# A fourth tile of 128 tokens takes its experts by gathers, and the dense 512 tokens become one span

## The chip, the cores and the metric

The kernel runs on one core of a Trainium2 chip. The metric is the time of one execution on the device, in microseconds (us); the median of the runs counts. A profile of one execution comes with it.

## The reference

One step of an encoder layer for 1024 prompt tokens and 32 sample tokens (1056 together), model width 1024, in fp32. It has sparse and forgetting attention, cross-attention into 256 memory tokens, and at the end a mixer that looks up experts, which is the part that the change touches:

```python
def peer_ffn(xn, w_q, keys1, keys2, u, v):      # cut
    def blk(xb):                                 # xb: 128 tokens
        q = (xb @ w_q).reshape(TOK_BLOCK, 8, 256)
        s1 = einsum('thd,hnd->thn', q[..., :128], keys1)   # 8 heads x 128 keys
        s2 = einsum('thd,hnd->thn', q[..., 128:], keys2)
        v1, i1 = top_k(s1, 16);  v2, i2 = top_k(s2, 16)
        ...                                      # the best 16 of the 256 pairs, per head
        eidx = ...                               # i1 * 128 + i2: one of 16384 experts
        g = softmax(sv)
        h = gelu(einsum('td,thkd->thk', xb, u[eidx]), approximate=False)
        return einsum('thk,thkd->td', g * h, v[eidx])
```

So each token picks 8 x 16 = 128 experts. An expert is one row of 1024 numbers in `u` and one in `v`; both tables have 16384 rows (64 MB each).

## The kernel before

The mixer computes the same thing in two ways. For the *dense* tokens TensorE multiplies all 16384 experts, 128 at a time (a *chunk*; there are 128 chunks), and a gate that is zero for the experts that a token did not pick weighs the result. For the *sparse* tokens GpSimd gathers, for each token, the 128 rows that it picked, by one indirect DMA (128 rows x 4 KB = 0.524 MB) from `u` and later one from `v`. Three tiles of 128 prompt tokens and the 32 sample tokens are sparse. The sample tokens are laid out four ways, so that 32 tokens x 128 experts take 32 gathers as well, and `NSP` = 3 x 128 + 32 = 416 gathers are made from each table. The other `ND` = 640 tokens are dense, and TensorE takes them in two spans (`NGD` = 2) of `TD` = 320 columns.

Operands of the dense products are split in two fp32r parts, and three matmuls (`PRODUCTS`) stand for one. Per chunk and span that is 8 x 3 = 24 matmuls.

Four stages matter, with each engine running its own instruction list, all tied by semaphores:

1. `peer_queries` computes the queries. At its end ScalarE and GpSimd split the dense columns of the normed input into `xd` (L1254, L1217).
2. `route` (1757 to 2788 us). Nine tiles in the order `ORDER` (sparse ones and the sample tile first) go through VectorE, which picks the best 16 keys and pairs in 20 ordered steps. Meanwhile TensorE works on the dense hidden values (`DenseHidden`): SyncE loads a chunk of `u` (0.524 MB) into one of two buffers (`load`), ScalarE rounds it (`round`, L1310), GpSimd subtracts to get the low part (`split`, L1314), TensorE multiplies (`product`, L1326), ScalarE applies Gelu (L1337), SyncE stores the result to `s_hid`. Also meanwhile GpSimd gathers rows of `u` into 8 row buffers (`gather`, L1567) and VectorE makes a dot product of each row set with the token (`dot`, L1598), in nine slots between its first steps of a tile. `CHUNKS_AT[j]` and `DOTS_AT[j]` say how many chunks and dots stand beside tile j. GpSimd's list for a tile is, per chunk, one split and then gathers up to a goal that is 4 ahead of an even spread. In the last chunk of stage j ScalarE first waits for VectorE's tile j - 1 (`dd_ready`, `Exp` at L1543), and TensorE waits for its indices at the end of the stage (`turn`, L1480), so the lists meet once per tile. Gathers begin in stage 2, after the chunks of stages 0 and 1. After the last `Exp`-marked tile 32 dots remain.
3. `spread_gates` (2788 to 3065 us, with the last store landing near 3097). For each dense token VectorE makes two one-hot matrices (L1916, L1921), TensorE multiplies them to a 128 x 128 gate (L1879), ScalarE copies four tokens at a time to `g_stage` (L1934), SyncE stores 128 tokens at once (8.4 MB) to `s_gate`. There are two stage buffers. Beside it the first 24 batches (`B_STEPS`) of the sparse sum run: GpSimd gathers four token rows of `v` (L1788), TensorE adds them (`SparseSum.sum`, L1821: 16 matmul records a batch).
4. `experts` (3115 to 4268 us). 32 phases of four chunks. SyncE loads `v`, the stored hidden values and the gates of a chunk (two buffers each); ScalarE and GpSimd round and split `v` (L2101, L2142); VectorE multiplies hidden by gate (L2176), ScalarE rounds, VectorE splits (L2181). These run one phase ahead of TensorE, which multiplies four outputs at a time over the four chunks (L2080) into four PSUM banks; VectorE adds them to `y` (L2216). Between groups TensorE takes the remaining 80 batches of sparse rows (L1821), at positions from `slot_of`. GpSimd gathers those rows (L1788) into `NBUF` = 11 buffers, two batches ahead of the sums.

## Time and profile before

| | us |
|---|---|
| median of 3 runs (4300.76 to 4316.1) | 4309.61 |
| the profiled execution | 4316.03 |
| its span, first to last instruction | 4314.1 |

| engine | busy us | share of the span |
|---|---|---|
| TensorE, matmul (PE) | 3830.1 | 89% |
| TensorE, weight load (PEld, beside PE) | 3166.4 | 73% |
| VectorE (DVE) | 2510.5 | 58% |
| ScalarE (ACT) | 995.8 | 23% |
| GpSimd (POOL) | 1604.4 | 37% |

The DMA engines moved 835.35 MB, of which 436.26 MB in the queue that GpSimd's gathers use and 371.29 MB in that of SyncE's direct DMAs. Busy shares are averages over the whole span; the stages have different limits. Times in rows are from the start of the span. A matmul's record lasts longer than the distance to the next one, since matmuls are pipelined: distances, not durations, give its cost. A few records are missing in the trace. PEclk 1.00 is the full clock of 2.4 GHz, 0.50 is 1.2 GHz.

### The profile page before, as it was taken

How to read it: one execution, taken by the hardware profiler on the slowest of the kernel's cores; microseconds unless marked ns; L12 is line 12 of the kernel's file. 1: busy time of each engine (PE TensorE's matmuls, PEld its weight loads, DVE VectorE, ACT ScalarE, POOL GpSimd, SP SyncE). 2: the span in 40 equal slices, each digit the busy share in tenths (PEclk: the TensorE clock that was granted, in tenths of full speed). 3: DMA queues.
4: the chain of work that ended last, by engine and by line, in shares of the span. 5: the costliest groups of instructions: out<-in, count | busy, mean ns of one | idle time of the engine just before them, and what ended most of it. 6: DMA issues, size and time to landing. Idle time of an engine off the chain costs nothing. (4 is left out here: it accounts for less than half of the span.)

```text
span 4314.1 us, 61852 instructions
## 1 busy us (share of the span) xinstructions
PE 3830.1 (89%) x22675; PEld 3166.4 (73%) x22691; DVE 2510.5 (58%) x6016; ACT 995.8 (23%) x1843; POOL 1604.4 (37%) x1134
## 2 busy tenths in 40 slices
PE   7878888888899989899999999787499999999996
PEld 4445665665567689899999999765378888888885
DVE  3878883330124142489999989898444544444444
ACT  1213332330102010322222222233222211211121
POOL 0000000000000033377777778646265655555551
PEclk9889998999999999999999999899799999999998
DMA  2010000003110132499999899789887887787772
GB/s 102 13 48 17 16 7 10 10 13 135 49 49 11 34 114 79 138 340 336 329 331 339 320 357 386 298 280 348 271 304 280 304 289 287 277 295 277 278 278 97
DMA packets 334637, 835.35 MB, mean 194 GB/s; under 512 B 28496, under 2 KB 130776, under 8 KB 332480
## 3 DMA queue, kind: packets, MB, share of 16 engines
q0 software_dynamic: 119808, 436.26, 26.9%
q1 hardware_dynamic: 210128, 371.29, 24.8%
q10 hardware_dynamic: 4464, 24.66, 1.4%
q8 instruction: 147, 2.41, 0.2%
q14 instruction: 90, 0.74, 0.1%
HBM read 722.74 MB, written 109.36 MB: 193 GB/s over the span
## 5 line engine op out<-in xcount | busy, mean ns | idle before, releaser
L2080 PEld LDWEIGHTS e_y_ps<-e_wh,e_vh 128*128 128x128 f32 x6144 | 918.3, 191 | 180.6 <-issue 94.2
L2080 PE MATMUL e_y_ps<-e_wh,e_vh 128*128 128x320 f32 x6144 | 953.8, 315 | 100.0 <-DVE e_wh L2181 60.3
L1326 PE MATMUL h_ps<-xd,h_uh 128*128 128x320 f32 x6144 | 925.0, 312 | 2.1 <-POOL h_uh L1314 2.0
L1326 PEld LDWEIGHTS h_ps<-xd,h_uh 128*128 128x128 f32 x6144 | 916.3, 191 | 5.8 <-POOL h_uh L1314 5.0
L1209 POOL CAST q_wh<-q_w 128x1024 fp32r<-128x1024 f32 x16 | 18.4, 1148 | 1634.8 <-DMA q_w<-in_w_pq 1528.6
L2216 DVE TENSOR_TENSOR oT<-e_y_ps,oT 128x320 f32<-128x320 f32 x512 | 231.6, 486 | 612.7 <-PE e_y_ps L2080 511.7
L1598 DVE CUSTOM_DVE_ANT_0 oT<-oT,r_row_ps 128x1024 f32<-128x1024 f32 x416 | 490.8, 1215 | 115.9 <-DMA oT<-in_u,eid 97.7
L2142 POOL TENSOR_TENSOR e_vh<-e_v,e_vh 128x1024 fp32r<-128x1024 f32 x128 | 318.8, 2493 | 449.7 <-ACT e_vh L2101 448.7
L1567 POOL DMA_INDIRECT oT<-in_u,eid x416 | 410.9, 988 | 123.6 <-issue 97.1
L1314 POOL TENSOR_TENSOR h_uh<-h_u,h_uh 128x1024 fp32r<-128x1024 f32 x128 | 327.5, 2559 | 180.4 <-ACT h_uh L1310 172.1
L197 PE MATMUL m_ps<-oT,m_w 128*128 128x352 f32 x1152 | 346.2, 464 | 21.1 <-DVEq L203 20.5
L1788 POOL DMA_INDIRECT e_rows<-in_v,idt x320 | 319.6, 999 | 91.7 <-issue 75.5
L197 PEld LDWEIGHTS m_ps<-oT,m_w 128*128 128x128 f32 x1152 | 221.0, 192 | 145.4 <-DVEq L203 21.9
L1337 ACT ACTIVATE h_hid<-h_ps 128x320 f32<-128x320 f32 x256 | 111.2, 437 | 626.2 <-PE h_ps L1326 492.3
L2106 ACT ACTIVATE e_wh<-e_hid 128x640 fp32r<-128x640 f32 x128 | 94.2, 737 | 627.3 <-DVE e_hid L2176 589.9
L1879 PE MATMUL g_ps<-g_hot 128*128 128x128 f32 x1280 | 177.2, 288 | 51.1 <-DVE g_hot L1921 50.5
L1879 PEld LDWEIGHTS g_ps<-g_hot 128*128 128x128 f32 x1280 | 154.7, 193 | 89.1 <-DVE g_hot L1921 66.3
L1236 PE MATMUL q_ps<-q_xh,q_wh 128*128 128x352 f32 x1152 | 186.0, 324 | 11.3 <-POOL q_wh L1211 11.3
L1236 PEld LDWEIGHTS q_ps<-q_xh,q_wh 128*128 128x128 f32 x1152 | 185.8, 190 | 11.8 <-issue 11.8
L1788 POOL DMA_INDIRECT oT<-in_v,idt x96 | 148.9, 1551 | 109.8 <-PE z_ps L1821 87.1
L2176 DVE TENSOR_TENSOR e_hid<-e_hid,e_gate 128x640 f32<-128x640 f32 x128 | 146.9, 1148 | 60.8 <-DMA e_gate<-s_gate 60.8
L1921 DVE TENSOR_SCALAR g_hot<-con,routes 128x128 f32<-128x128 f32 x640 | 179.9, 360 | 0.0
(272 smaller groups left out, 4768.5 us busy)
## 6 DMA issues: line engine op xcount, KB each, us to landing
h_u<-in_ut SPq DMA_DIRECT2D x128, 512.0 KB
e_v<-in_v SPq DMA_DIRECT2D x128, 512.0 KB
s_hid<-h_hid SPq DMA_DIRECT2D x128, 320.0 KB
s_gate<-g_stage SPq DMA_DIRECT2D x5, 8192.0 KB
e_hid<-s_hid SPq DMA_DIRECT2D x128, 320.0 KB
e_gate<-s_gate SPq DMA_DIRECT2D x128, 320.0 KB
s_pq<-q_out ACTq DMA_DIRECT2D x16, 528.0 KB, 2.7
q_w<-in_w_pq SPq DMA_DIRECT2D x16, 512.0 KB, 3.5
```

What stands on the lines that cost most here:

```text
L197: mm = pe.matmul(self.ps[:, b * n + g, 0:c], self.wbuf[:, b, k, :], self.src[:, k, a:a + c], start=(k == 0), stop=(k == KD - 1))
L1236: mm = pe.matmul(ps[:, b, g, 0:TG], wh[:, b, hw, k * P:(k + 1) * P], xh[:, hx, k, g * TG:(g + 1) * TG], start=(k == 0 and n == 0), stop=(k ...
L1314: pool.tensor_tensor(self.uh[:, n % 2, LO, :], self.u[:, n % 2], self.uh[:, n % 2, HI, :].bitcast(F32), ALU.subtract).then_inc(self.split_ ...
L1326: mm = pe.matmul(self.ps[:, bank % 3, 0:TD], self.uh[:, n % 2, a, k * P:(k + 1) * P], self.xd[:, b, k, g * TD:(g + 1) * TD], start=(k == 0 ...
L1567: pool.indirect_dma_start(out=rows[:, n % N_ROW, :], out_offset=None, in_=dram["u"], in_offset=bass.IndirectOffsetOnAxis(ap=eid[:, n:n + 1 ...
L1598: dve.tensor_tensor_reduce(out=rows[:, d % N_ROW, :], in0=rows[:, d % N_ROW, :], in1=row_flat, scale=1.0, scalar=0.0, op0=ALU.mult, op1=AL ...
L1788: pool.indirect_dma_start(out=buffer, out_offset=None, in_=self.rows_dram, in_offset=bass.IndirectOffsetOnAxis(ap=self.idt[:, col:col + 1] ...
L1879: mm = pe.matmul(ps[:, q % 4, x, :], hot2[:, q % 4, x, :], hot1[:, q % 4, x, :], start=True, stop=True)
L1921: op = dve.tensor_scalar(hot1[:, g, x, :], iota, routes[:, 0, tok], routes[:, 2, tok], ALU.is_equal, ALU.mult)
L2080: mm = pe.matmul(y_ps[:, o, 0:TD], vh[:, n % SLOT, a, m * P:(m + 1) * P], wh[:, n % SLOT, b, g * TD:(g + 1) * TD], start=(c == 0 and e == ...
L2142: pool.tensor_tensor(vh[:, n % SLOT, LO, :], v[:, n % 2, :], vh[:, n % SLOT, HI, :].bitcast(F32), ALU.subtract).then_inc(v_split, 1)
L2216: dve.tensor_tensor(y[:, m, cols], y_ps[:, o % 4, 0:TD], y[:, m, cols], ALU.add).then_inc(y_added, 1)
```

## The change

`NS` goes from 3 to 4: a fourth tile of 128 prompt tokens is sparse. 512 dense tokens are left, and they form one span of 512 columns (`TD, NGD = ND, 1`), so that each weight is used by one matmul of 512 columns where two of 320 used it. There are 544 gathers from each table instead of 416: 128 more dots in `route`, and 112 instead of 80 batches of the sparse sum in `experts` (the 24 in `spread_gates` stay). `route` gets new lists: stages 2 to 9 have 14 chunks each, stages 1 to 8 have 64 dots each. `spread_gates` makes four stores instead of five; the stage buffers change places, so that the first store goes into buffer 1. The turned weights of the sample tokens go to a PSUM bank of their own, since 544 columns don't fit in one, and ScalarE copies them by two instructions. In `experts` there are 8 outputs in a phase instead of 16, VectorE adds two per chunk (was four), the sums of sparse rows may follow every second chunk of a group, and `NBUF` is 13.

```diff
-NS = 3
+NS = 4
 C0 = NS * P
 ND = T_P - C0
-TD, NGD = ND // 2, 2
+TD, NGD = ND, 1
...
-CHUNKS_AT = (2, 6, 13, 13, 13, 13, 13, 13, 17, 17, 8)
+CHUNKS_AT = (3, 10, 14, 14, 14, 14, 14, 14, 14, 14, 3)
-DOTS_AT = (0, 43, 43, 42, 43, 43, 42, 64, 64, 32)
+DOTS_AT = (0, 64, 64, 64, 64, 64, 64, 64, 64, 32)
...
-            act.wait_ge(self.kept, 1)
+            act.wait_ge(self.kept, 2)
...
-        assert NB % 2 == 1
-        keep["gates_stored"] = (stored[0], 16 * (NB // 2 + 1))
+        assert NB % 2 == 0
+        keep["gates_stored"] = (stored[1], 16 * (NB // 2))
...
-                             stage[:, n % 2]).then_inc(stored[n % 2], 16)
-            sp.wait_ge(stored[1], 16 * (NB // 2))
+                             stage[:, 1 - n % 2]).then_inc(stored[n % 2], 16)
+            sp.wait_ge(stored[0], 16 * (NB // 2))
...
-                    mm = pe.matmul(sums.ps[part, 1, 0, C0:NSP], hn[:, C0:NSP], ident[:, part],
+                    mm = pe.matmul(sums.ps[part, 1, 1, 0:T_S], hn[:, C0:NSP], ident[:, part],
...
-                act.activation(stage[:, n % 2, :, q % NQ * 4:q % NQ * 4 + 4], ps[:, q % 4].rearrange("p x a -> p a x"),
+                act.activation(stage[:, 1 - n % 2, :, q % NQ * 4:q % NQ * 4 + 4], ps[:, q % 4].rearrange("p x a -> p a x"),
                                ACT.Copy).then_inc(copied, 1)
...
-                    act.activation(sums.wt[:, :], sums.ps[:, 1, 0, 0:NSP], ACT.Copy).then_inc(sums.kept, 1)
+                    act.activation(sums.wt[:, 0:C0], sums.ps[:, 1, 0, 0:C0], ACT.Copy).then_inc(sums.kept, 1)
+                    act.activation(sums.wt[:, C0:NSP], sums.ps[:, 1, 1, 0:T_S], ACT.Copy).then_inc(sums.kept, 1)
...
-NBUF = 11
+NBUF = 13
...
-                    for s in steps_in(p, b0 // 4):
-                        if s in TURNS:
-                            turn_sum(TURNS.index(s))
-                        else:
-                            sparse_sum(batch_at(s))
+                        if c % 2 == 0:
+                            continue
+                        for s in steps_in(p, b0 // 2 + c // 2):
+                            if s in TURNS:
+                                turn_sum(TURNS.index(s))
+                            else:
+                                sparse_sum(batch_at(s))
...
-                    for o in range(4 * i, 4 * i + 4):
-                        if p + 1 < NPH and o == 4 * i:
+                    for o in range(2 * i, 2 * i + 2):
+                        if p + 1 < NPH and o == 2 * i:
                             weigh(n)
-                        if p + 1 < NPH and o == 4 * i + 2:
+                        if p + 1 < NPH and o == 2 * i + 1:
                             split(n)
```

## Rows read from the trace of the kernel before

**Rows 1.** Stretches: us, busy time (count) of each engine, PEclk, DMA share, GB/s.

```profile
1757.40:2788.50 1031.10, 954.76 (x6427) 948.56 (x6427) 909.88 (x2805) 280.33 (x454) 738.39 (x546) 0.96 0.88 325
2788.50:3065.30 276.80, 224.78 (x1678) 165.99 (x1678) 258.96 (x795) 97.74 (x175) 147.41 (x95) 0.97 0.88 304
3115.20:4268.00 1152.80, 1102.79 (x7489) 958.81 (x7489) 518.81 (x773) 226.39 (x292) 628.76 (x444) 0.98 0.76 277
```

**Rows 2.** Timeline of ScalarE, the routing tiles' marks: start us, us, instruction, idle before.

```profile
1919.83 0.31 ACT L1543 ACTIVATE r_eg<-r_dd 128x128 f32<-128x128 f32 x1 [11.33 <-DVE r_dd L1691]
...
2442.37 0.31 ACT L1543 ACTIVATE r_eg<-r_dd 128x128 f32<-128x128 f32 x1 [11.66 <-DVE r_dd L1691]
...
2579.14 0.31 ACT L1543 ACTIVATE r_eg<-r_dd 128x128 f32<-128x128 f32 x1 [14.86 <-DVE r_dd L1691]
...
2713.85 0.31 ACT L1543 ACTIVATE r_eg<-r_dd 128x128 f32<-128x128 f32 x1 [15.00 <-DVE r_dd L1691]
```

**Rows 3.** Waits from 2579 to 2713.8: us in total, times, longest us.

```profile
POOL h_uh L1314 <- ACT h_uh L1310: 11.2, 1, 11.2
```

**Rows 4.** Groups by line, routing stage: count | busy us, mean ns | idle before.

```profile
L1567 POOL DMA_INDIRECT oT<-in_u,eid x416 | 410.9, 988 | 123.6 <-issue 97.1 <-DVE hn L1598 22.0
L1314 POOL TENSOR_TENSOR h_uh<-h_u,h_uh 128x1024 fp32r<-128x1024 f32 x127 | 325.2, 2560 | 159.8 <-ACT h_uh L1310 151.5 <-issue 6.9
```

**Rows 5.** Timeline: gate stage of VectorE, and ScalarE's first expert row.

```profile
3051.94 0.69 DVE L1916 TENSOR_TENSOR g_hot<-con,routes 128x512 f32<-128x512 f32 x1
...
3053.56 0.69 DVE L1916 TENSOR_TENSOR g_hot<-con,routes 128x512 f32<-128x512 f32 x1
...
3097.66 1.06 ACT L2101 ACTIVATE e_vh<-e_v 128x1024 fp32r<-128x1024 f32 x1 [32.39 <-DMA e_v<-in_v]
```

**Rows 6.** Timeline of the expert stage, TensorE: three groups of 48 and two sums.

```profile
3311.37 14.56 PE L2080 MATMUL e_y_ps<-e_wh,e_vh 128*128 128x320 f32 x96
3325.86 1.92 PE L1821 MATMUL z_ps<-e_rows,z_wz 128*32 128x512 f32 x16
...
3336.91 0.41 PE L2080 MATMUL e_y_ps<-e_wh,e_vh 128*128 128x320 f32 x1
```

**Rows 7.** Timeline of the routing stage, ScalarE: one chunk's two Gelus.

```profile
2494.77 0.44 ACT L1337 ACTIVATE h_hid<-h_ps 128x320 f32<-128x320 f32 x1 [2.19 <-PE h_ps L1326]
2498.23 0.44 ACT L1337 ACTIVATE h_hid<-h_ps 128x320 f32<-128x320 f32 x1 [3.02 <-issue]
```

**Rows 8.** A stretch of the query stage, L1236 alone (352 columns): PE, PEld, PEclk, DMA.

```profile
1540.00:1580.00 40.00, 40.00 (x253) 40.00 (x253) 1.00 0.27 93
```

**Rows 9.** Timeline of VectorE in routing: a tile's end and eight dots.

```profile
2578.82 0.28 DVE L1691 TENSOR_TENSOR r_dd<-r_sv 128x128 f32<-128x128 f32 x1
...
2601.20 1.20 DVE L1598 CUSTOM_DVE_ANT_0 oT<-oT,r_row_ps 128x1024 f32<-128x1024 f32 x1
...
2610.31 0.08 DVE L1662 MATCH_VALUE_LOAD r_pick<-r_v,r_s 128x8 f32 x1
```

**Rows 10.** Stretches as in rows 1: a routing tile in two parts, gates, experts' start.

```profile
2578.00:2604.00 26.00, 25.04 (x152) 24.73 (x153) 25.49 (x46) 8.51 (x15) 19.42 (x11) 0.88 0.60 205
2604.00:2702.00 98.00, 97.81 (x663) 96.86 (x662) 87.55 (x291) 25.75 (x41) 83.08 (x67) 1.00 1.02 400
2850.00:2990.00 140.00, 120.74 (x928) 88.22 (x920) 140.00 (x432) 52.32 (x95) 82.92 (x57) 1.00 1.08 381
3110.00:3130.00 20.00, 7.08 (x24) 6.34 (x24) 4.22 (x4) 2.10 (x3) 1.16 (x1) 0.50 0.80 305
```

**Rows 11.** The gathers of routing, one line: duration ns min/median/max, first and last start us.

```profile
L1567 POOL DMA_INDIRECT oT<-in_u,eid x416: 932/938/2212, 1828.6 to 2775.8; - x139
```

**Rows 12.** Waits of the gate stage: us in total, times, longest us.

```profile
DVE g_hot L1916 <- PE g_ps L1879: 15.9, 1, 15.9
```

**Rows 13.** Groups by line, whole span, expert stage: columns as in rows 4.

```profile
L1788 POOL DMA_INDIRECT e_rows<-in_v,idt x320 | 319.6, 999 | 91.7 <-issue 75.5 <-PE z_ps L1821 9.6
L2142 POOL TENSOR_TENSOR e_vh<-e_v,e_vh 128x1024 fp32r<-128x1024 f32 x128 | 318.8, 2493 | 449.7 <-ACT e_vh L2101 448.7
```

## Prediction

> **What bounds the kernel now.** I read the busy time of each engine by stage first [rows 1]. The edit touches three stages: the routing stage (1757.4 to 2788.5 us), the gate stage (to 3065.3) and the expert stage (3115.2 to 4268.0). TensorE is busy 93% and 96% of the first and last, so narrow views have to say whether it is also what sets their pace.
>
> Routing works in tiles; one `Exp` on ScalarE marks each [rows 2]. Tiles with 42 or 43 dot products and 13 chunks are 104.5 us apart (five intervals between the first two rows), the two with 64 and 17 are 136.8 and 134.7 us apart. Inside the last one GpSimd waits only once, 11.2 us [rows 3]; a gather costs it 0.988 + 0.276 = 1.26 us (mean duration, and 97.1 us of issue gaps over 352), a weight split 2.56 us [rows 4]. 17 x 2.56 + 64 x 1.26 + 11.2 = 135.4 us: GpSimd's queue alone gives the measured tile. The 11.2 us lie between its last gather of a tile and the next split: rows land, VectorE finishes the dots, then `Exp`, Gelu and the rounding on ScalarE. TensorE waits for VectorE there too. In 13-chunk tiles GpSimd needs 33.3 + 54 + 11 = 98 us and TensorE about as much, and 104.5 us come out.
>
> In the gate stage VectorE never rests: its step for 4 tokens repeats every 1.63 us [rows 5]. The expert stage is TensorE's: 8.5 us per slot of 48 matmuls and 2/3 of a row sum [rows 6].
>
> **Change, routing stage.** Each tile now has 64 dots and 14 chunks.
> - TensorE: 48 matmuls of 320 columns become 24 of 512. Gelu follows Gelu by 3.46 us in the rows shown and by 3.52 on average of a chunk's two, per 24 matmuls [rows 7]: 146.5 ns each. 253 matmuls of 352 columns fill 40 us: 158 ns [rows 8]. That slope (0.36 ns a column) gives 216 ns at 512, one cycle a column of 2.4 GHz gives 226; I take 226, as both rows sit 11 to 13 ns above their columns. A chunk falls from 7.04 to 5.42 us.
> - GpSimd: 14 x 2.56 + 64 x 1.26 + 11.2 = 127.7 us a tile.
> - VectorE: eight dots from 2601.20 to 2610.31, 1.14 us each, 73 us; the rest of a tile about 48 us, of which 22.4 stand in one piece without dots (2578.8 to 2601.2) [rows 9]. 121 us.
> - DMA: 64 gathers x 0.524 MB + 14 x (0.524 + 0.262) + 1.05 = 45.6 MB. The engines carry 400 GB/s for the 98 us in which dots run, and 5.3 MB in the 26 us around the piece without dots [rows 10]. 26 + 40.3/0.400 = 127 us.
>
> Three resources lie within 7 us of each other, and TensorE, with 76 + 13 us, is out. I take 128.5 us a tile, bounds 125 and 136 (the 17-chunk tiles, whose sum met the measured time without a surplus).
>
> Gathers begin once 14 chunks instead of 9 are through: 14 x 5.42 against 9 x 7.04 us, +12.5, with one more tile of x rows turned first (8 matmuls and a copy) +14.5: first gather at 1843 instead of 1828.6 [rows 11]. From it to the first tile's `Exp` took 91.2 us [rows 2]; 20 more gathers and a split make it 119, so 1962. Seven tiles x 128.5 end at 2861.5. Then 19 us of VectorE without dots, 32 dots x 1.14, 5 of waits, 3.3 to the next stage: 64, so 2925.5. **Routing: +137 us** (bounds +112, +190).
>
> **Change, gate stage.** 160 steps become 128. VectorE: 32 x 1.63 = -52. But the 96 gathers stay and are squeezed: a batch of four (2.1 MB) every 4.5 steps, 7.3 us, is 286 GB/s, and this stage saturates at 381 [rows 10]; 95 are left for the stores of 8.4 MB, one per 52 us. All bytes (83.9 MB) less the 10 of the first 52 us need 194 us, so 246 us; VectorE's chain with the last store (27 us) needs 235. From the stage's start to the first expert row now: 310 us (to 3098) [rows 5], with one wait of 15.9 us of VectorE in it [rows 12], behind a late gather. I take 250: **-60 us** (bounds -68, -40).
>
> **Change, expert stage.**
> - TensorE: 144 matmuls and 2 sums take 25.5 us, a sum 1.86 us, so 151 ns a matmul [rows 6]. Now 6144 x 0.151 + 80 x 1.86 + 10 = 1087 of 1152.8 us. After: the overhead above the columns (17.7 ns) kept, 231 ns: 3072 x 0.231 + 112 x 1.86 + 12 = 930.
> - GpSimd: 448 gathers x 1.24 + 124 splits x 2.49 = 865 us (now 706) [rows 13].
> - DMA: gathers 235 MB, v 67, hidden and gates 67, y 4: 373 MB (now 323 at 280 GB/s). At 400 GB/s 932 us.
> - VectorE: 128 weigh/split pairs at (0.61 + 0.69) and 256 adds at 0.6: 320 us. No bound. In a group of four outputs its order (add, split, add, weigh, add, split, add, 4.4 us from the first output, which is there 2.05 us before the group's end) is some 0.4 us late for the fourth bank; a sum in between covers it in most groups.
>
> So 932, 930 and 865 replace one leader with 1087. Today's loss above the leader is 66 us, about 20 of it the cold start. Where three were equal before (13-chunk tiles, 98 each) 7% came on top. 930 x 1.07 + 20 = 1015; DMA has to hold 92% of its best rate here if nothing else stalls, more than in any tile, so I take 1031 (362 GB/s on average, what the 17-chunk tiles held). **-122 us** (bounds -200 at the floors, -35 if DMA averages 335 GB/s as in the 13-chunk tiles).
>
> The ring of 13 rows (was 11) and the moved PSUM columns cost nothing; `xd` splits are shorter by 2.4 us before the stage, hidden by the extra turned tile.
>
> The Trainium skill (DMA: Bandwidth & Descriptors, Specifications) gives a core a limit of about 358 GB/s at the HBM. The 400 GB/s over 98 us, mostly reads of tables there, stand against it [rows 10]. By the rule the expert stage could not be under 373/0.358 = 1042 us, the total not under 4276, and case A below could not be.
>
> **Sum.** Profiled execution 4316.0 us: +137 - 60 - 122 = -45, 4271. The median shown is 6.4 below that execution: 4265.
>
> **Rivals.**
> A. The expert stage overlaps nearly ideally (950 to 990 us). For: thirteen row buffers and a phase of slack between load and use. Taken at 970: 4265 - 61 = 4204.
> B. Slower: DMA decides the expert stage. TensorE waits in order for gathered rows between dense groups; in the trace no sum of that stage waits for DMA, at 76% DMA share, so nothing shows how it behaves near 100%. Each late batch delays the dense groups, their release of v and hidden buffers, and so the next loads. At 335 GB/s the stage takes 1114 us: 4348. It decides from 343 GB/s downwards (1088 us, at which the total is 4322, 0.3% slower).
> C. Routing tiles stay at 135 to 136 us, because VectorE's two-input steps stretch GpSimd's gathers and DMA waits add: +52, 4317, no change.
> D. TensorE's clock. In routing it would be busy 5.4 of every 8.3 us. At 86% busy in the gate stage it is granted 2.4 GHz, at 35% (3110 to 3130) 1.2 [rows 10]; between them no row speaks. At 1.2 GHz a chunk takes about 10.3 us and a tile 158: +235 us, 4500. Against: a slow chunk keeps TensorE busy without a gap. The Trainium skill (TensorE: Matmul & The Clock Gate, A second HAM failure mode: psum-queue depth-cycling) tells of a kernel in which short pauses between groups of matmuls let the clock swing between its levels; by that this case would come, in part at least.
>
> **How the numbers follow.** Forecast case (4215 to 4295) 0.47; A 0.16; B 0.17; C 0.13; D 0.03; 0.04 unforeseen. 0.3% is about what a measurement can tell from no change. A and the forecast and a part of C are faster: 0.69. C's rest and the edges: same 0.12. B, D and what is unforeseen: slower 0.19. Range 4190 to 4345: it takes in A and most of B, and leaves out D and the worst of B.
>
> **What would show it.** `Exp` marks 126 to 131 us apart and the first at 1962; gate-stage matmuls starting near 2926; expert stage 1000 to 1065 us with a DMA share above 0.9 and TensorE waiting for gathered rows; matmuls of 512 columns 226 to 231 ns apart. Wrong, if tiles are 121 or 136 us, or if the expert stage is under 1000 or over 1088 us.

## The result and the profile after

The changed kernel takes 4364.5 us (median; 4362.0 to 4368.2), the kernel before 4310.0 beside it. The ratio is 1.0139 (95% interval 1.0120 to 1.0158): it is 1.4% slower, where 4265 was forecast, and outside the range. Its profiled execution took 4365.3 us with a span of 4363.3.

Both spans divide at the same marks: first dense matmul of the routing stage, first matmul of the gate stage, first dense matmul of the expert stage, last one.

| stage, us | before | after | difference | forecast |
|---|---|---|---|---|
| routing | 1031.1 | 1192.8 | +162 | +137 |
| gates, to the first expert matmul | 326.7 | 284.6 | -42 | -60 |
| experts | 1151.8 | 1079.8 | -72 | -122 |
| sum | | | +48 | -45 |

So the median lies 99 us above the forecast: 50 of them are in the expert stage, 25 in routing, 18 in the gates; the rest is mostly that this profiled execution lies 0.8 us above its median, where the forecast took 6.4 off.

The first view is busy time by stage, as in [rows 1] (start:end, length, then busy us and instructions of PE, PEld, DVE, ACT, POOL, and PEclk, DMA share, GB/s): routing, the gate stage's matmuls, 10 us inside them, the expert stage, and last the seven routing tiles between first and last `Exp`.

```profile
1758.80:2951.60 1192.80, 857.94 (x3356) 663.04 (x3356) 1075.28 (x3042) 246.97 (x327) 855.10 (x675) 0.87 0.88 330
2951.60:3186.00 234.40, 196.11 (x1424) 139.30 (x1424) 207.66 (x635) 77.69 (x143) 117.43 (x95) 0.93 0.91 323
3070.00:3080.00 10.00, 2.26 (x11) 2.29 (x11) 0.06 (x1) 2.25 (x5) 0.00 (x0) 0.50 1.08 342
3236.20:4316.00 1079.80, 1025.17 (x4944) 637.98 (x4944) 356.88 (x518) 220.13 (x309) 735.08 (x572) 0.99 0.91 342
1964.05:2887.40 923.35, 665.43 (x2566) 510.99 (x2565) 866.49 (x2451) 189.98 (x251) 685.56 (x546) 0.87 0.91 343
```

In the last row VectorE is busy 94% of the tiles, TensorE 72%, GpSimd 74%, and no engine is at 100%. In the expert row TensorE is busy 1025 of 1080 us, yet the floor forecast for its work was 930. A matmul that waits once it has begun counts as busy: the records of the sums (L1821) fill 291 us of this row, and 226 in lead3 below, where the same sums find their rows.

The tiles' marks, answering to [rows 2]: (2887.41 - 1964.05) / 7 = 131.9 us a tile.

```profile
1964.05 0.31 ACT L1543 ACTIVATE r_eg<-r_dd 128x128 f32<-128x128 f32 x1 [21.32 <-DVE r_dd L1691]
...
2887.41 0.31 ACT L1543 ACTIVATE r_eg<-r_dd 128x128 f32<-128x128 f32 x1 [20.82 <-DVE r_dd L1691]
```

Groups of the page, answering to [rows 4] and [rows 13]: count | busy us, mean ns | idle before and its releaser.

```profile
L1567 POOL DMA_INDIRECT oT<-in_u,eid x544 | 538.4, 990 | 185.8 <-issue 119.8
L1788 POOL DMA_INDIRECT e_rows<-in_v,idt x448 | 438.4, 979 | 119.7 <-issue 106.5
...
L2145 POOL TENSOR_TENSOR e_vh<-e_v,e_vh 128x1024 fp32r<-128x1024 f32 x128 | 306.3, 2394 | 247.7 <-ACT e_vh L2104 246.1
L1314 POOL TENSOR_TENSOR h_uh<-h_u,h_uh 128x1024 fp32r<-128x1024 f32 x128 | 316.4, 2472 | 166.1 <-ACT h_uh L1310 164.3
```

GpSimd's prices are close to the forecast's (gathers 0.98 to 0.99 us, splits 2.4 to 2.5). So its counts and prices were right, and what came on top is order and waiting. The waits from 3180 to 4320 us (us in total, times, longest us) name the first such thing.

```profile
POOL e_vh L2145 <- ACT e_vh L2104: 246.1, 59, 46.4
...
PEld z_ps L1821 <- DMA e_rows<-in_v,idt: 104.8, 76, 2.6
...
PE z_ps L1821 <- DMA e_rows<-in_v,idt: 44.5, 51, 1.7
...
POOL e_rows L1788 <- PE z_ps L1821: 5.5, 18, 0.3
```

TensorE's weight loads wait for gathered rows in 76 places, 104.8 us in total. The 51 waits of its matmuls begin at the same moments and are the same waits, so they are not added (the 149 us of the expectation of lead3 counts them twice). Before, no wait of that stage was for rows. GpSimd, which issues these gathers, hardly waits for a free row buffer (5.5 us), but 246 us for ScalarE's rounding, 198 of them inside the stage. The chain of waits of 80 us in mid-stage (start, us, what) shows how the two hang together:

```profile
3516.32 2.03 PE z_ps L1821 x16
...
3518.38 0.24 ACT z_wz L1802
...
3518.78 1.05 ACT e_vh L2104
...
3519.90 2.40 POOL e_vh L2145
...
3522.44 0.95 POOL e_rows L1788
...
3527.43 2.40 POOL e_vh L2145
...
3532.75 0.94 POOL e_rows L1788
...
3533.99 9.42 DMA e_rows<-in_v,idt
...
3543.45 1.90 PE z_ps L1821 x10
3545.36 5.71 PE e_y_ps L2081 x24
```

A sum ends at 3518.35. ScalarE had waited for it, since after every fourth batch it places the weights of a later four; its next instruction rounds `v`, GpSimd splits that, gathers a batch, splits again, gathers the next, and that one's last row lands 9.4 us later, at 3543.41. From the end of the sum to the landing 25.1 us pass. The row belongs to the third sum after. TensorE's own timeline there (start, us, what, [idle before]):

```profile
3516.25 2.09 PE L1821 MATMUL z_ps<-e_rows,z_wz 128*32 128x512 f32 x16
...
3523.93 2.74 PE L1821 MATMUL z_ps<-e_rows,z_wz 128*32 128x512 f32 x16
...
3532.27 2.68 PE L1821 MATMUL z_ps<-e_rows,z_wz 128*32 128x512 f32 x16
...
3540.57 1.96 PE L1821 MATMUL z_ps<-e_rows,z_wz 128*32 128x512 f32 x6
3543.45 1.90 PE L1821 MATMUL z_ps<-e_rows,z_wz 128*32 128x512 f32 x10 [0.92 <-DMA e_rows<-in_v,idt]
3545.29 5.78 PE L2081 MATMUL e_y_ps<-e_wh,e_vh 128*128 128x512 f32 x24
3550.99 1.92 PE L1821 MATMUL z_ps<-e_rows,z_wz 128*32 128x512 f32 x16
3552.85 5.78 PE L2081 MATMUL e_y_ps<-e_wh,e_vh 128*128 128x512 f32 x24
```

Where nothing waits, a sum follows the last one after 7.6 us (3543.45 to 3550.99: 1.85 for the sum, 5.70 for 24 dense matmuls). So between the end of a sum and the fourth row of the third sum after TensorE has three dense groups, two sums and three eighths of one, 21.5 us of work, and the row comes after 25.1. The missing 3.6 us are waits. As an estimate from these rows, 28 such rounds of four batches lose 28 x 3.6 = 101 us. In the kernel before, the same three sums lie 39 to 46 us apart (for example sums at 3623.04 and 3661.95).

### The profile page after: what moved, and what is told of

Same layout as the page of the kernel before. It is cut to its first block and busy times, and to the rows that moved or that the text cites. A ratio compares the mean times of both kernels' runs of the same rounds, so it can differ in the third digit from the quotient of the medians.

```text
span 4363.3 us, 50039 instructions
## 1 busy us (share of the span) xinstructions
PE 3640.8 (83%) x16837; PEld 2539.1 (58%) x16837; DVE 2466.6 (57%) x5860; ACT 937.3 (21%) x1703; POOL 1795.1 (41%) x1390
## 5 line engine op out<-in xcount | busy, mean ns | idle before, releaser
L1326 PE MATMUL h_ps<-xd,h_uh 128*128 128x512 f32 x3072 | 826.9, 430 | 183.1 <-POOL h_uh L1314 183.1
L1326 PEld LDWEIGHTS h_ps<-xd,h_uh 128*128 128x128 f32 x3072 | 629.1, 208 | 372.3 <-POOL h_uh L1314 222.3
L2081 PE MATMUL e_y_ps<-e_wh,e_vh 128*128 128x512 f32 x3072 | 742.4, 397 | 59.9 <-DVE e_wh L2184 56.2
L2081 PEld LDWEIGHTS e_y_ps<-e_wh,e_vh 128*128 128x128 f32 x3072 | 570.1, 189 | 279.0 <-issue 133.7
L1598 DVE CUSTOM_DVE_ANT_0 oT<-oT,r_row_ps 128x1024 f32<-128x1024 f32 x544 | 641.2, 1215 | 112.2 <-DMA oT<-in_u,eid 106.7
L1567 POOL DMA_INDIRECT oT<-in_u,eid x544 | 538.4, 990 | 185.8 <-issue 119.8
L1788 POOL DMA_INDIRECT e_rows<-in_v,idt x448 | 438.4, 979 | 119.7 <-issue 106.5
L2219 DVE TENSOR_TENSOR oT<-e_y_ps,oT 128x512 f32<-128x512 f32 x256 | 175.7, 687 | 519.2 <-PE e_y_ps L2081 519.2
L1821 PE MATMUL z_ps<-e_rows,z_wz 128*32 128x512 f32 x1792 | 291.1, 606 | 44.7 <-DMA e_rows<-in_v,idt 44.5
L2179 DVE TENSOR_TENSOR e_hid<-e_hid,e_gate 128x512 f32<-128x512 f32 x128 | 115.7, 904 | 237.9 <-DMA e_gate<-s_gate 237.9
L1236 PE MATMUL q_ps<-q_xh,q_wh 128*128 128x352 f32 x1152 | 186.1, 324 | 11.3 <-POOL q_wh L1211 11.3
L1236 PEld LDWEIGHTS q_ps<-q_xh,q_wh 128*128 128x128 f32 x1152 | 185.8, 190 | 11.8 <-issue 11.8
L1821 PEld LDWEIGHTS z_ps<-e_rows,z_wz 128*32 128x32 f32 x1792 | 58.6, 109 | 212.5 <-issue 106.7
```

The source lines that it names most:

```text
L1236: mm = pe.matmul(ps[:, b, g, 0:TG], wh[:, b, hw, k * P:(k + 1) * P], xh[:, hx, k, g * TG:(g + 1) * TG], start=(k == 0 and n == 0), stop=(k ...
L1326: mm = pe.matmul(self.ps[:, bank % 3, 0:TD], self.uh[:, n % 2, a, k * P:(k + 1) * P], self.xd[:, b, k, g * TD:(g + 1) * TD], start=(k == 0 ...
L1567: pool.indirect_dma_start(out=rows[:, n % N_ROW, :], out_offset=None, in_=dram["u"], in_offset=bass.IndirectOffsetOnAxis(ap=eid[:, n:n + 1 ...
L1598: dve.tensor_tensor_reduce(out=rows[:, d % N_ROW, :], in0=rows[:, d % N_ROW, :], in1=row_flat, scale=1.0, scalar=0.0, op0=ALU.mult, op1=AL ...
L1788: pool.indirect_dma_start(out=buffer, out_offset=None, in_=self.rows_dram, in_offset=bass.IndirectOffsetOnAxis(ap=self.idt[:, col:col + 1] ...
L1821: mm = pe.matmul(self.ps[g * 32:(g + 1) * 32, t % 2, half, :], self.wz[:, b // 4 % 2, b % 4 * P + g * 32:b % 4 * P + (g + 1) * 32], buffer ...
```

## The experiments

All are edits of the changed kernel unless another is named. Four came first, each taking away one resource in both big stages.

**half_gather.** Each gather of the two stages moves 128 rows of 2 KB instead of 4, and the upper half of every row buffer holds zeros. The table is read as one of half rows, so that index e now points at a half of row e // 2: the values are of other experts, and the addresses lie in half of the table, while counts and bytes are as meant. The gathers from `v` are edited likewise.

```diff
-                pool.indirect_dma_start(out=rows[:, n % N_ROW, :], out_offset=None, in_=dram["u"],
+                pool.indirect_dma_start(out=rows[:, n % N_ROW, 0:D // 2], out_offset=None,
+                                        in_=dram["u"].rearrange("n (h d) -> (n h) d", h=2),
```

> The changed kernel, but each gather of the routing and expert stages moves 2 KB per expert instead of 4 (half rows; the rest of the row buffers holds zeros, so experts' results are wrong in both stages); all instruction counts stay. Routing tile 131.9 us now (28.9 MB instead of 45.6), expert stage 1080 us (256 MB instead of 373). Theory 'DMA rate': both stages are held by the bytes. Then a tile falls to VectorE's 121 to 124 us, and the expert stage to TensorE's 940 to 970 us. Theory 'lists': GpSimd's list (split, then gathers, lock-step with ScalarE and VectorE) holds them; then the tile stays at 128 to 131 us, and the expert stage at 1030 us or more, since the latency of a gather but not its place in the list changes.

**short_split.** GpSimd's subtractions touch 8 instead of 1024 columns, so the rest of the low parts of `u` and `v` is that of the first chunks. `v`'s split is edited likewise.

```diff
-        pool.tensor_tensor(self.uh[:, n % 2, LO, :], self.u[:, n % 2], self.uh[:, n % 2, HI, :].bitcast(F32),
+        w = D if n < 2 else 8
+        pool.tensor_tensor(self.uh[:, n % 2, LO, 0:w], self.u[:, n % 2, 0:w], self.uh[:, n % 2, HI, 0:w].bitcast(F32),
```

> The changed kernel, but GpSimd's low-part splits cover 8 of 1024 columns after the first use of each buffer (2.4 us each become about 0.1), in routing and experts; the low parts are stale. Bytes are the same. Theory 'lists': GpSimd has 34 us less in a tile and 2.4 us less ahead of every four gathers in the expert stage: the tile falls to VectorE's 122 to 126 us, the expert stage from 1080 to 960 to 1010 us. Theory 'DMA rate': tile 129 to 131 us, expert stage not under 1050.

**half_dots.** VectorE's dots run over the first 512 of 1024 columns, the rest is left out of them.

```diff
-                dve.tensor_tensor_reduce(out=rows[:, d % N_ROW, :], in0=rows[:, d % N_ROW, :], in1=row_flat,
+                dve.tensor_tensor_reduce(out=rows[:, d % N_ROW, 0:D // 2], in0=rows[:, d % N_ROW, 0:D // 2],
+                                         in1=row_flat[:, 0:D // 2],
```

> The changed kernel, but VectorE's dot products in routing read 512 of the 1024 columns (about 0.6 us each instead of 1.14, 35 us less in a tile; the hidden values of sparse tokens are wrong). If VectorE sets the tile (121 of 131.9 us): it falls to the next of GpSimd and DMA, 127 us, or less if the 8 us in which GpSimd waits for row buffers go. If DMA or GpSimd's list sets it: 127 to 131 us. The expert stage stays at 1080.

**one_product.** TensorE makes one dense product of three; the two with a low part are left out (8 matmuls for 24, in both stages).

```diff
+FEW = ((HI, HI),)
...
-                for o, (a, b) in enumerate(PRODUCTS):
+                for o, (a, b) in enumerate(FEW):
```

> The changed kernel, but TensorE makes one of the three split products in the dense parts of routing and experts (8 matmuls a chunk instead of 24; results have lower precision). TensorE is then at 1.8 us a chunk in routing and 240 + 220 us in the expert stage. If TensorE (992 of 1080 us busy) still holds the expert stage, it falls by several hundred us to the DMA floor of 930; if the loop of row sums, ScalarE's placing, GpSimd's list and the gather's landing holds it, it falls by less than 120 us and stays above 960. Routing: unchanged at 130 to 132 us a tile.

One execution of each, beside one of before at 4294.4:

| | us | routing | tile | experts |
|---|---|---|---|---|
| changed kernel (median, and its profile) | 4364.5 | 1192.8 | 131.9 | 1079.8 |
| half_gather | 4256.2 | 1163.0 | 128.9 | 998.6 |
| short_split | 4242.8 | 1140.5 | 125.8 | 1009.1 |
| half_dots | 4326.9 | 1159.7 | 127.8 | 1078.9 |
| one_product | 4284.4 | 1169.5 | 131.7 | 1022.8 |

Busy time of the expert stage, in the columns of the first view: half_gather, short_split, one_product.

```profile
3208.20:4206.80 998.60, 977.19 (x4943) 631.54 (x4944) 399.57 (x518) 218.96 (x309) 744.17 (x573) 0.99 0.74 252
3184.40:4193.50 1009.10, 985.57 (x4944) 636.28 (x4944) 333.41 (x518) 220.76 (x309) 464.32 (x572) 0.99 0.95 366
3209.50:4232.30 1022.80, 792.06 (x2896) 281.84 (x2896) 406.25 (x516) 219.66 (x309) 737.47 (x572) 0.90 0.95 361
```

Taking bytes away gives 81 us, taking GpSimd's splits away gives 71 with every byte still moved, and two thirds of the dense matmuls only 57. None alone is the bound. All three shorten the same loop: half rows land sooner (4.6 us after their issue, for 7.2, by the medians), short splits let gathers go sooner, a faster TensorE ends its sums sooner. In routing TensorE gives 0.2 us a tile, dots 4.1 for 34 us of VectorE, splits 6.1 for 34 us of GpSimd, bytes 3.0. The expert stage of half_gather lies between what the two theories of its expectation had named (970 and 1030), so it decided for neither.

**two_spans.** One part of the change undone: two spans of 256 columns, the expert loops as before (48 matmuls a group, 4 outputs a chunk), the fourth sparse tile kept.

```diff
-TD, NGD = ND, 1
+TD, NGD = ND // 2, 2
```

> The changed kernel with the 512 dense tokens in two spans of 256 columns, and the expert loops as before (16 outputs a phase, four adds per chunk, sums after every group): the fourth sparse tile without the single span. TensorE: 256 columns at about 124 ns against 119 ns per half of a 512 matmul: 6144 x 0.124 + 208 + 12 = 982 us in the expert stage against 992 now. Forecast: routing tile unchanged (TensorE is out of it), expert stage 1080 to 1110 us, total 4360 to 4400 us. If the single span itself is what costs (longer adds, fewer banks in flight), it would be faster than the changed kernel by over 15 us.

Ratio to before 1.0098 (1.0071 to 1.0126), 4348.2 us. Tiles 132.5, experts 1065.4: the longer matmuls bring nothing in the changed kernel; two spans are 14 us better there. 16 us in all is more than the 15 that the expectation took as the sign that the single span itself costs time; lead3_two below shows that it doesn't once rows come in time. Why two spans lose less to late rows stays open.

**lead3.** GpSimd gathers three batches ahead of TensorE in the expert stage instead of two. The 13 row buffers stay.

```diff
-goal = min(batch_at(steps_before(p, i)) + 2, N_BATCH)
+goal = min(batch_at(steps_before(p, i)) + 3, N_BATCH)
```

> The changed kernel; in the expert stage GpSimd gathers three batches ahead of the sums instead of two (13 row buffers hold three batches and one row). Theory 'late order': TensorE waits 149 us for gathered rows because they are ordered only two batches ahead, 8 to 9 us before use, with a landing time of 7 us: the expert stage falls from 1080 to 1000 to 1030 us, total 4290 to 4320. Theory 'DMA rate': the rows are late because the DMA engines are full; the stage stays within 15 us of 1080.

Ratio 0.9911 (0.9887 to 0.9935), 4268.3 us. The expert stage takes 983.8 us instead of 1079.8 with the same instructions and bytes, more than the 50 to 80 us expected; routing is as it was (131.7). One line takes the kernel from slower than before to faster. (That its 4268 is near the forecast's 4265 is chance: routing and gates are 43 us above their forecasts, the expert stage 46 under.)

```profile
3237.20:4221.00 983.80, 964.48 (x4943) 628.05 (x4944) 383.62 (x518) 222.67 (x309) 748.55 (x572) 0.99 0.97 375
```

Its waits for rows are nearly gone, 7.0 us for 104.8; the difference is 98 us, and the stage is 96 us shorter:

```profile
PEld z_ps L1821 <- DMA e_rows<-in_v,idt: 7.0, 10, 1.8
```

**exp_late.** In the last chunk of a routing stage ScalarE does the chunk's Gelu and the next rounding ahead of its wait for VectorE and `Exp`, so that GpSimd would get a split at the tile's end.

```diff
+                    if last:
+                        hidden.gelu(act, n)
+                        if n + 2 < NKEY:
+                            hidden.round(act, n + 2)
                         act.wait_ge(dd_ready, j)
```

> The changed kernel; in routing ScalarE does the last chunk's Gelu and the next rounding before it waits for VectorE's tile and takes Exp, so that GpSimd doesn't stand for 11 us at each tile's end. Theory 'GpSimd list' (34.6 + 80.6 + 11 + 8 us of waits = the tile): a tile falls from 131.9 to 123 to 126 us, total 4300 to 4325. Theory 'VectorE and DMA': the eight row buffers are full anyway while VectorE makes no dots, and the tile stays at 129 to 132.

Ratio 1.0131 (1.0106 to 1.0156), tile 131.1: 0.8 us a tile, and 4 us by the medians, which the intervals don't tell from nothing. GpSimd still waits 87.6 us for ScalarE's rounding in the seven tiles (81.8 in the changed kernel), so the order of ScalarE's list alone doesn't give it the split early; what holds it there stays open.

**both** joins lead3 and exp_late.

> lead3 and exp_late in one kernel. The stages are apart in time, so the gains should add: each theory expects the sum of its two single values within 5 us.

Ratio 0.9892 (0.9867 to 0.9917), 4259.8 us; tile 130.9, experts 982.5.

**lead3_two** is lead3 with the two spans of two_spans.

> lead3 (gathers three batches ahead) with two spans of 256 columns instead of one of 512. With rows ordered two batches ahead the two spans took 1065 us in the expert stage against 1080 with one, so the single span had no worth there. If TensorE's work sets the stage once the rows are in time (965 of 984 us busy), two spans cost 6144 x 0.124 against 3072 x 0.233 = +46 us: 1010 to 1035 us, total 4295 to 4320. If DMA sets it (375 GB/s), both are equal within 15 us.

Ratio 0.9949 (0.9933 to 0.9966), tile 132.4, experts 1001.5. With the rows in time, one span is worth 18 us in the expert stage (983.8 against 1001.5), less than the 26 to 51 expected if TensorE sets the pace; with rows late it cost 14.

**lead1** goes the other way: one batch ahead (`+ 1`).

> The changed kernel with gathers only one batch ahead of the sums in the expert stage (two in the changed kernel, three in lead3; bytes and instructions the same). Theory 'late order': every batch then meets its own landing time of 7 us and the stage grows by over 150 us beyond 1080. Theory 'DMA rate': no change.

4724.8 us in one execution; the expert stage takes 1434.1, and the waits for rows are 273 us:

```profile
PEld z_ps L1821 <- DMA e_rows<-in_v,idt: 272.6, 175, 4.9
```

1434.1 / 112 is 12.8 us a sum. At two ahead it is 9.6, at three 8.8. The steps are -354 and -96 us, and with 7.0 us of waits left at three, a fourth batch has little to take.

**lead3_half** is lead3 with the half rows.

> lead3 with gathers of 2 KB per expert instead of 4 in routing and experts (as half_gather; results of the sparse tokens are wrong). Expert stage now 984 us with 373 MB. If DMA's rate sets it (379 GB/s), half the gathered bytes give TensorE's floor: 945 to 955 us. If TensorE sets it already, it stays within 10 us.

4229.7 us in one execution; tile 128.9, experts 969.8 at 260 GB/s. Half the bytes give 14 us now, where they gave 81 at two ahead. The expectation had 945 to 955 us for a stage held by DMA and under 10 us of change for one held by TensorE; the result lies between, nearer the second.

**lead3_light** adds the short splits to that, to see what is under GpSimd and DMA in routing.

> lead3_half and short_split together (2 KB gathers; GpSimd's splits of 8 columns): in a routing tile only VectorE's list is untouched, TensorE's is short of it. If VectorE's list is the floor of the tile, the tile is 121 to 124 us (131.9 now, 125.8 with short splits alone, 128.9 with half gathers alone). Below 120 it would not be VectorE's. Expert stage as lead3_half within 5 us.

4132.1 us in one execution; tile 117.8, experts 967.9. Its seven tiles, in the columns of the first view:

```profile
1947.80:2772.10 824.30, 626.80 (x2566) 487.19 (x2565) 820.50 (x2452) 190.19 (x251) 476.45 (x546) 0.89 0.74 242
```

VectorE is busy 820.5 of 824.3 us: that is its own time for the same dots and picks, 117.8 us a tile. The expectation had put it at 121 and said that a tile under 120 would not be VectorE's; the busy time shows that it is, and that 121 holds only beside the splits: in the changed kernel these instructions take 866.5. Bytes alone give 3.0 us a tile, splits alone 6.1, both together 14.1: each stands behind the other. Where they are gone, GpSimd waits for VectorE's row buffers instead of VectorE for rows. The waits of the seven tiles (us in total, times, longest us), three of the changed kernel, then one of lead3_light, from 1960 to 2800 us:

```profile
POOL h_uh L1314 <- ACT h_uh L1310: 81.8, 7, 12.3
POOL oT L1567 <- DVE hn L1598: 57.0, 86, 2.8
DVE oT L1598 <- DMA oT<-in_u,eid: 49.4, 63, 2.4
```

```profile
POOL oT L1569 <- DVE hn L1605: 149.8, 71, 7.0
```

**gates_half** halves the bytes of the gate stage's gathers alone, on top of lead3, as half_gather does elsewhere; the upper half of those buffers keeps old values.

> lead3, but the 96 gathers of the gate stage move 2 KB per expert instead of 4 (half rows; the sparse sum of the first 24 batches is wrong). From the gate stage's first matmul to its last takes 234 us in the changed kernel, where VectorE's 128 steps of 1.63 us need 208. Theory 'DMA': gathers and stores of 8.4 MB share 385 GB/s, stores return their buffer late and ScalarE, TensorE and VectorE wait in turn. Then it falls to 208 to 214 us. Theory 'order': the sums, closer together, hold TensorE whatever the bytes; then it stays above 225.

In its one execution the gate matmuls run from 2950.8 to 3167.1, 216.3 us; 234.4 in the changed kernel (233.5 in lead3), where VectorE is busy 207.7. So 17 to 18 of the 27 us above VectorE go with these bytes, fewer than the theory 'DMA' expected (208 to 214 us in all) and more than the other. The place where they show is the return of the stage buffer (first the wait in the changed kernel, then the page's line of the stores: count, KB, us to landing):

```profile
ACT g_stage L1934 <- DMA s_gate<-g_stage: 34.1, 2, 18.5
```

```profile
s_gate<-g_stage SPq DMA_DIRECT2D x4, 8192.0 KB, 66.8
```

In lead3 that wait is 30.7 us, in gates_half it is gone. VectorE stands twice behind it in the changed kernel, for 13 us around 3075 (the third row of the first view) and 10 around 3137, together 23 of the 27.

**rows10** is both with ten row buffers in routing (8 before) and gathers six ahead of an even spread (4 before).

```diff
-LEAD = 4
+R_ROW = 10
+LEAD = 6
...
-                if n >= N_ROW:
-                    pool.wait_ge(dotted, n - N_ROW + 1)
+                if n >= R_ROW:
+                    pool.wait_ge(dotted, n - R_ROW + 1)
```

> The kernel 'both' with ten row buffers in routing instead of eight, and gathers six ahead instead of four. Theory: VectorE's 22 us without dots leave the DMA engines idle because the eight buffers are full, and GpSimd waits about 8 us a tile for VectorE to free one; two more rows (1.05 MB, 2.6 us of DMA) take 2 to 4 us off each tile: 130.9 to 127 to 129, total 4260 to 4230 to 4250. Rival: VectorE's own list (121 us) and its meetings with ScalarE hold the tile; then under 1 us a tile and the total stays within 10 us.

Ratio 0.9814 (0.9798 to 0.9830), 4231.3 us: the fastest kernel here that leaves nothing out, 1.9% under before. Tile 128.2, beside 128.5 forecast, experts 983.5.

**before_rows9** gives the kernel before the routing edits of rows10: exp_late's order, and nine buffers with a lead of five.

> The kernel before with the orders of 'rows10' in routing, as far as memory allows (ScalarE's rounding ahead of its wait for the tile; nine row buffers instead of eight, gathers five ahead). It asks whether the kernel before gains as much from them: the routing tile of the changed kernel fell from 131.9 to 128.2 us by ten. If the tile of before (104.5 us for 43 dots) is held by TensorE's chunks (91.5 us) and its 7 us wait, it falls by under 1 us; the two 64-dot tiles (136.8, 134.7) are GpSimd's and fall by 3 to 8 us each. Total 4309 to 4290 to 4305.

Ratio 0.9980 (0.9967 to 0.9993), 4297.0 us: 9 us. Its 43-dot tiles take 103.4 us (104.5 before), its two 64-dot tiles 133.9 and 132.3 (136.8 and 134.7): 2.6 us each, where 3 to 8 were expected, and where rows10 takes 3.7 off each of the changed kernel's with one buffer more. So part of rows10's gain the kernel before would have had as well, in the two tiles it has of that kind; against before_rows9 rows10 is 1.5% faster. Three batches ahead weren't tried on the kernel before: no wait of its expert stage is for rows, so there is little for them to take.

## Why the prediction was wrong

**Experts, forecast -122, measured -72: the step that failed is the one from 930 to 1031.** TensorE's floor (930), DMA (932) and GpSimd (865) were compared as amounts of work, and a surplus was taken from how the 13-chunk tiles had behaved. None of the terms held the distance, in time, between a gather and the sum that needs it. From rows of before and the program it could have been worked out. The loop from the end of a sum to the landing of the row for the third sum after holds two splits (5) and two batches of gathers (10), by [rows 4] and [rows 13], and ScalarE's placing and rounding (1.5) and the landing (9.4), by the chain of after: 26 us, 25.1 in the chain itself. At the forecast's own prices TensorE needs 3 x 24 x 0.231 + 2.4 x 1.86 = 21 us from there to that row (21.5 in the trace), and in the kernel before, where the sums are fewer and each group is longer, the three sums spread over 39 to 46 us. 39 cover the loop, 21 don't. The mean interval hides it: 9.2 us a sum in a stage of 1031 us would make 3 x 9.2 = 28, but the sums come 7.6 us apart with gaps elsewhere. lead3 lets the row be ordered one sum earlier, lead1 one later: lead1, the changed kernel and lead3 are three points of that one cause (12.8, 9.6, 8.8 us a sum), by one number in one line. What was measured in the place of 1031 is 1079.8, with 105 us of waits for rows.

**Rival B had the symptom and not the cause.** It named TensorE's waits in order for gathered rows, and it put the deciding point at 343 GB/s and 1088 us; the stage ran at 342 GB/s and 1079.8 us. But the rate is mostly the result of the lateness. lead3 moves the same bytes at 375 GB/s; half_gather, with 252 of 369 MB (0.68, from the views' GB/s and lengths) at a DMA share of 0.74, still took 0.92 of the time. As a limit on bytes a second Rival B is refuted, though its time (4348) was the nearest of all; bytes count in that a half row lands 2.6 us sooner.

**The floor itself was low.** lead3_half still needs 969.8 us with its rows in time and 260 GB/s. The matmul of 512 columns was forecast at 226 in routing and at 231 ns here; 24 of them end 5.73 us after they start in the expert stage, 5.87 in routing, less the last one's own 0.39 us about 232 and 238:

```profile
3510.59 5.73 PE L2081 MATMUL e_y_ps<-e_wh,e_vh 128*128 128x512 f32 x24
```

So inside a group the price was right to 1 ns here. But from the start of a group to the start of the sum behind it 5.70 us pass (3545.29 to 3550.99; 5.71 in lead3_half as well), not 24 x 0.231 = 5.54: over 128 groups that is 21 of the 40 us of lead3_half above 930. The other half stays open; the slow start of the stage is part of it. Rival A (950 to 990) is what lead3 gives with 983.8; as a forecast for this kernel it was wrong.

**Routing, forecast +137, measured +162.** The first `Exp` (1964 for 1962) and the tail after the last (64.2 for 64) came as worked out. The tile is 131.9 for 128.5, 24 us over seven. The step that failed is the list of resources: three within 7 us of each other were named (127.7, 127, 121), and the largest plus 1 us was taken. They don't overlap freely, since they hand 8 row buffers round. GpSimd waited 57 us in the tiles for VectorE to free one, beside 11.7 us a tile at its end (81.8 / 7, forecast 11.2); VectorE waited 49 us for rows. More buffers and a longer lead together (rows10, 2.7 us under both) brought 128.2; with GpSimd and DMA relieved, VectorE alone needs 117.8 (forecast 121), and beside them its instructions take 866.5 / 7 = 123.8. Rival C (135 to 136) did not come.

**VectorE's two-input steps.** The prediction priced VectorE and GpSimd apart. But GpSimd's splits make VectorE's own list longer: the same instructions of VectorE take 866.5 us in the seven tiles of the changed kernel and 833.6 in those of short_split, where the splits are nearly gone and DMA moves more, 360 GB/s:

```profile
1959.10:2839.90 880.80, 633.98 (x2566) 492.45 (x2565) 833.63 (x2451) 194.32 (x252) 472.62 (x546) 0.87 0.93 360
```

Two lines hold the whole difference of 33 us: the 14 additions of L1671 on 128 columns, which last 1.5 us each beside splits and 0.28 without, and the 7 of L1718, 2.48 and 0.29. So 4.7 of the 6.1 us a tile of short_split are VectorE's, and only the rest is GpSimd's queue. The Trainium skill (SBUF — State Buffer, Who interferes with whom) says that VectorE's second port is shared with GpSimd under an exclusive lock, and that DMA has ports of its own. The trace is in line with it, since the 33 us go with the splits and not with the bytes; that it is the port no run shows by itself. Between short_split and lead3_light another 13 us of busy time go with the bytes. At least part of that is how busy time is counted: the dots last 1.21 us each in both, and where one follows another without a wait their records overlap.

**Gates, forecast -60, measured -42.** The forecast took 250 us from the stage's start to the first expert row. With 2951.6 as its start and 3219.3 as that row it is 268. The step that failed is VectorE's chain, put at 208 + 27 = 235 with no wait in it: the 208 became 234.4, and the last store took 33 for 27. The missing term is again a buffer's return: a store of 8.4 MB lands 67 us after its issue, and with gathers beside it ScalarE stood twice for it (34 us) and VectorE behind ScalarE (23 us).

**Rival D, the clock.** It did come in part, and cost the tile nothing. Chunks of 24 matmuls, one view of the routing stage (start, us, what, [idle before]):

```profile
2122.97 8.23 PE L1326 MATMUL h_ps<-xd,h_uh 128*128 128x512 f32 x24 [3.65 <-POOL h_uh L1314]
2131.47 5.87 PE L1326 MATMUL h_ps<-xd,h_uh 128*128 128x512 f32 x24 [0.27 <-POOL h_uh L1314]
...
2147.19 7.42 PE L1326 MATMUL h_ps<-xd,h_uh 128*128 128x512 f32 x24 [2.59 <-POOL h_uh L1314]
```

The second is granted 1.00, 2.4 GHz; the first and third, which follow idle pieces of 3.65 and 2.59 us, are granted 0.68 and 0.77 and are stretched, and the clock granted in the tiles is 0.87 on average, a mix of 1.00 and 0.50. The tiles have 9.4 us for a chunk, so even 8.23 fits, and a third of the matmuls (one_product) leaves the tile at 131.7. The Trainium skill (TensorE: Matmul & The Clock Gate, A second HAM failure mode: psum-queue depth-cycling) describes such swings in a kernel that lost throughput by them; the trace agrees on the swing, and shows no loss here, where TensorE does not set the tile.

## What to carry to other kernels

A prefetch distance counted in steps shrinks in time when the steps get faster or denser. Find the whole loop, from the consumer's release through every engine queued in between to the landing, count which later step needs what is ordered there, and set the loop against the time to that step where steps are closest, not against the mean. Floors of engines and DMA can all fit and the stage still lose 96 us to one number in a line. Busy shares hide such waits where a started instruction counts as busy, and a wait that stands in the weight load's row and in the matmul's is one wait. Where several resources that share a ring of buffers lie within a few per cent, relieving one gives a fraction of what is removed (34 us of splits gave 6.1), and even that may be another engine's instructions getting shorter (4.7 of the 6.1). The ring's depth and lead cost no work and gave 2.7 more.

## What the runs showed of the hardware

- DMA held 375 GB/s over the 984 us of lead3's expert stage, gathers and direct loads mixed, at a DMA share of 0.97. The Trainium skill (DMA: Bandwidth & Descriptors, Specifications) gives about 358 GB/s for a core at the HBM, as half of a stack's 716 GB/s. Taken as the limit of this one core, as the prediction took it, the 369 MB of the stage (375 GB/s over 983.8 us) would need at least 0.369 / 0.358 = 1031 us (an estimate by that figure); it took 983.8, so here the half share did not bind. Whether the kernel drew on the other core's half no run shows.
- The landing of a gather of 128 rows of 4 KB (8.5 and 9.4 us in the chain, 7.2 by the median of the stage, 4.6 with rows of 2 KB) is as long as 1.5 groups of 24 matmuls, 5.7 us each, and GpSimd's work for it is 0.95 us and 0.30 of issue.
- TensorE's clock swings between its two levels in routing at 72% busy, chunk by chunk (5.87 to 8.23 us for the same 24 matmuls), while over the expert stage, busy 95%, 0.99 is granted.
- GpSimd's subtractions on 128 x 1024 hold two kinds of VectorE's two-input additions: 1.5 us for 0.28 (L1671) and 2.48 for 0.29 (L1718), while the other large groups of VectorE's list last the same with and without them.
